# Two-layer decoder trunk on one core: the normalized stream by a diagonal product, products bank by bank, router and weight parts in another order

## What is computed

```python
h = rmsnorm(x, g) * (1.0 + scale) + shift   # rmsnorm: x * rsqrt(mean(x*x) + EPS) * g
x = x + gate * f(h)
# MoE: router logits, sigmoid, best 4 of 8 groups, best 8 experts, weights normalized
scores = sigmoid(h @ router_w)
y = sum over chosen e of w_e * (silu(h @ w1[e]) * (h @ w3[e])) @ w2[e]
y = y + (silu(h @ s_w1) * (h @ s_w3)) @ s_w2
```

## Time and profile before

| | |
|---|---|
| median of 3 runs | 1453.29 us (1452.13 to 1454.12) |
| the profiled execution | 1451.76 us, span 1450.0 us |
| busy: PE, DVE, ACT, POOL | 1328.0, 550.8, 444.5, 206.1 us |
| mean granted clock of TensorE | 0.974 of full speed |
| HBM read | 514.10 MB, 355 GB/s over the span |

### The profile page before, as it was taken

One profiled execution on the slowest core, in us unless ns is written; L12 is line 12 of the kernel. 1 busy time (PEld: TensorE's weight loads), 2 busy tenths in 40 slices (PEclk: granted clock), 3 DMA queues, 4 the chain that ended last, 5 costly groups with the idle time before them and its releaser, 6 DMA issues.

```text
span 1450.0 us, 32945 instructions
## 1 busy us (share of the span) xinstructions
PE 1328.0 (92%) x12029; PEld 875.3 (60%) x12030; DVE 550.8 (38%) x1217; ACT 444.5 (31%) x874; POOL 206.1 (14%) x657
## 2 busy tenths in 40 slices
PE   4899678999999999998789999789999999999996
PEld 2788366555455554554489989665555555555553
DVE  2565457233232332222443445473233223322333
ACT  3443333222122222221334454332222222222222
POOL 8000021111111111111000000011111111111110
PEclk9899988999999999999889999999999999999999
DMA  9999992999999999999985534529999999999994
GB/s 345 372 381 399 409 352 81 423 419 423 422 421 422 422 421 422 423 421 421 383 281 181 169 117 146 189 107 422 420 422 421 422 421 422 421 422 422 422 421 204
DMA packets 113082, 516.06 MB, mean 356 GB/s; under 512 B 9368, under 2 KB 46368, under 8 KB 63104
## 3 DMA queue, kind: packets, MB, share of 16 engines
q1 hardware_dynamic: 109920, 509.64, 87.6%
q0 software_dynamic: 2400, 3.49, 0.8%
q10 hardware_dynamic: 704, 2.10, 0.4%
HBM read 514.10 MB, written 1.09 MB: 355 GB/s over the span
## 4 chain that ended last, share of the span: by engine, by line
PE 72%; SPq 8%; DVE 5%; ACT 5%; DMA 5%; issue 3%; POOL 1%; ACTq 1%; DVEq 0%; POOLq 0%
PE bank L882 20%; PE bank L1059 15%; PE bank L1062 7%; PE bank L1080 7%; PE bank L994 6%; PE bank L1035 5%; SPq L336 5%; DMA ring<-in_exp_w_dram 4%; PE bank L1086 3%; PE bank L858 2%; SPq L339 2%; DVE arena L1487 1%; ACT arena L674 1%; DMA ring<-in_da_w_out_dram 1%; PE bank L1069 1%
## 5 line engine op out<-in xcount | busy, mean ns | idle before, releaser
L1059 PE MATMUL bank<-ring,arena 128*64 128x512 f32 x768 | 178.5, 605 | 13.1 <-DMA ring<-in_exp_w_dram 13.1
L1035 PEld LDWEIGHTS bank<-arena 128*128 128x128 bf16 x3264 | 142.1, 98 | 55.5 <-issue 55.0
L994 PE MATMUL bank<-arena_r 128*128 128x512 f32 x560 | 161.1, 418 | 3.0 <-DVE arena_r L1499 3.0
L1499 DVE TENSOR_TENSOR arena_r<-bank,arena_r 128x512 fp32r<-128x512 f32 x136 | 94.1, 692 | 154.1 <-ACT arena_r L686 154.1
L1035 PE MATMUL bank<-arena 128*128 128x64 bf16 (+1 forms) x3264 | 151.8, 207 | 0.0
L679 ACT ACTIVATE arena<-bank 128x256 f32<-128x256 f32 (+1 forms) x68 | 22.6, 333 | 386.9 <-PE bank L1059 269.8
L686 ACT CAST arena_r<-bank 128x512 fp32r<-128x512 f32 x136 | 79.7, 586 | 189.5 <-PE bank L1080 124.8
L994 PEld LDWEIGHTS bank<-arena_r 128*128 128x128 f32 x560 | 94.6, 188 | 60.0 <-issue 47.5
L882 PE MATMUL bank<-HH_r,ring_r 128*128 128x256 f32 x448 | 127.7, 285 | 0.0
L531 POOL TENSOR_TENSOR arena<-arena,pass_base 128x2 f32 x136 | 23.6, 197 | 732.2 <-PE bank L1046 727.1
L1059 PEld LDWEIGHTS bank<-ring,arena 128*64 128x64 f32 x768 | 56.5, 139 | 114.5 <-issue 113.9
(11 more groups left out here) (271 smaller groups left out, 2151.2 us busy)
## 6 DMA issues: line engine op xcount, KB each, us to landing
ring<-in_exp_w_dram SPq DMA_DIRECT2D x264, 1024.0 KB, 24.0
ring<-in_ada_w_dram SPq DMA_DIRECT2D x48, 1024.0 KB, 12.3
HH<-in_exp_w_dram SPq DMA_DIRECT2D x40, 1024.0 KB, 20.4
mods<-in_exp_w_dram SPq DMA_DIRECT2D x40, 1024.0 KB, 24.3
arena<-in_exp_w_dram SPq DMA_DIRECT2D x40, 1024.0 KB, 25.0
ring<-in_ret_w_in_dram SPq DMA_DIRECT2D x24, 1024.0 KB, 11.2
ring<-in_da_w_in_dram SPq DMA_DIRECT2D x12, 1024.0 KB, 16.4
ring<-in_ret_w_out_dram SPq DMA_DIRECT2D x8, 1024.0 KB, 4.9
```

The lines of the kernel that those rows point to most:

```text
L994: ins = nc.tensor.matmul(banks[4 + NH * tc + hf][:, :], S[:, P * tc:P * tc + P], y[:, r, 512 * hf:512 * hf + 512], start=False, stop=(last ...
L1035: ins = nc.tensor.matmul(banks[2 - 2 * half][:, P * kk:P * kk + 2 * W], parts[:, tc, r, P * (4 * half + kk):P * (4 * half + kk + 1)], Pg[: ...
L1059: ins = nc.tensor.matmul(banks[1][W * i:W * i + W, :], xg[:, k, W * i:W * i + W], w13[j][:, k, :, :], start=(k == 0), stop=(k == KD - 1))
L1499: nc.vector.tensor_tensor(y[:, 1, 512 * hf:512 * hf + 512], banks[hf][:, :], y[:, 0, 512 * hf:512 * hf + 512], ALU.subtract).then_inc(u[f" ...
```

## The change

1. **Turn.** DVE no longer scales x. It writes `diag`, 128x128 per token block, the identity times `rs`, and `turn_h` makes 16 true f32 products of `X` (read with a step of 8 elements) with `diag`. The first of them waits for POOL's identity alone (`ident_ready`); `pool_consts` gates the second half of the first `ada` step.
2. **Bank by bank.** ACT and DVE evict, round and split bank after bank, and the first products (router, or the first half of the first projection) wait for two blocks of the width at a time (`hT_there(k)`). In the first place ACT evicts bank 3 too, and the low part of the first weight tile stands between evictions.
3. **Router and weight parts.** The router weights are rounded and split during the output projection before. The first shared or projection tile's low part is made during the turn. Sigmoid and silu tables are loaded by dummy activations.
4. **Parts of x.** They are made from `X` and `rs`, per token block: the high part around the sigmoid, the rest only after `route_ready`, the third part after `shT`.
5. **Ranks.** The rank products stand ahead of the third half of shared up, the placing products ahead of the fourth; the weights come after at_rank. POOL writes the limits from `chosen_ready` on and no longer clears `y`.

```diff
+        diag = ret_s[:, 0:TC * P].rearrange("p (c t) -> p c t", c=TC)
...
+                def round_high(m):
+                    if m in by_act:
+                        act.wait_ge(hT_act, (2 * n + 1 if n else 0) + by_act.index(m) + 1)
                     else:
-                        act.wait_ge(hT_dve, 2 * n + m // 2 + 1)
+                        act.wait_ge(hT_dve, (2 * n - 1 if n else 0) + by_dve.index(m) + 1)
                     nc.scalar.copy(hT_hi[:, 2 * m:2 * m + 2, :], hT_full[:, 2 * m:2 * m + 2, :]).then_inc(hT_rounded, 1)
+
+                act.wait_ge(mod_T_in[n], 1 if n == 0 else 16)
+                evict(0)
+                round_high(0)
+                evict(2)
+                round_high(1)
+                if n == 0:
+                    evict(3)
+                round_high(2)
+                round_high(3)
...
             def moe(l):
+                if l == 1:
+                    load_root_table()
                 round_w("shared", l, 0)
                 norm_stats()
-                act.wait_ge(late_consts_in, 16 * 5)
-                nc.scalar.copy(rw_hi, rw[:, :, :]).then_inc(rw_rounded, 1)
+                round_w("shared", l, 1)
+                nc.scalar.activation(lexp[:, 0:1], ident[:, 0:1], ACT.Sigmoid)
                 evict_hT()
-                round_w("shared", l, 1)
-                nc.scalar.copy(parts[:, :, 0, :], h).then_inc(part_hi, 1)
+
+                def part_high(tc):
+                    nc.scalar.activation(parts[:, tc, 0, :].rearrange("t (k p) -> t k p", k=KD),
+                                         X[:, tc, :].rearrange("t (p k) -> t k p", k=KD), ACT.Copy, scale=rs[:, tc:tc + 1]
+                                         ).then_inc(part_hi, 1)
+
+                part_high(0)
                 act.wait_ge(logits_done, l + 1)
-                nc.scalar.activation(scoreT, banks[2][:, 0:T], ACT.Sigmoid).then_inc(scoresT_ready, 1)
-
-                act.wait_ge(rest_ready, l + 1)
-                nc.scalar.copy(parts[:, :, 1, :], h).then_inc(part_mid, 1)
+                nc.scalar.activation(scoreT, banks[0][:, 0:T], ACT.Sigmoid).then_inc(scoresT_ready, 1)
+                part_high(1)
+                nc.scalar.activation(lexp[:, 0:1], ident[:, 0:1], ACT.Silu)
+                for tc in range(TC):
+                    act.wait_ge(rest_ready, TC * l + tc + 1)
+                    nc.scalar.copy(parts[:, tc, 1, :], h[:, tc, :]).then_inc(part_mid, 1)
...
             def turn_h():
                 for tc in range(TC):
-                    pe.wait_ge(h_ready, TC * norms[0] + tc + 1)
+                    pe.wait_ge(diag_ready, TC * norms[0] + tc + 1)
                     for m in range(4):
                         for kk in range(2):
-                            ins = nc.tensor.transpose(
-                                banks[m][:, T * kk + P * tc:T * kk + P * tc + P],
-                                h[:, tc, P * (2 * m + kk):P * (2 * m + kk + 1)], ident[:, :])
+                            ins = nc.tensor.matmul(banks[m][:, T * kk + P * tc:T * kk + P * tc + P],
+                                                   X[:, tc, :].rearrange("t (p k) -> t k p", k=KD)[:, 2 * m + kk, :],
+                                                   diag[:, tc, :], start=True, stop=True)
                         if tc == TC - 1:
                             ins.then_inc(h_turned, 1)
                 norms[0] += 1
 
-            def hT_there():
-                pe.wait_ge(hT_split, 4 * norms[0])
+            def hT_there(k):
+                if k % 2 == 0:
+                    pe.wait_ge(hT_split, 4 * (norms[0] - 1) + k // 2 + 1)
...
                 for k in range(KD):
+                    if i == 0 and m == 0:
+                        hT_there(k)
...
             def moe(l):
                 turn_h()
-                hT_there()
                 pe.wait_ge(rw_split, l + 1)
 
                 for k in range(KD):
-                    ins = product(banks[2][:, 0:T], (rw_hi[:, k, :], rw_lo[:, k, :]), [x[:, k, :] for x in hTs],
+                    hT_there(k)
+                    ins = product(banks[0][:, 0:T], (rw_hi[:, k, :], rw_lo[:, k, :]), [x[:, k, :] for x in hTs],
                                   k == 0, k == KD - 1)
                 ins.then_inc(logits_done, 1)
...
+                    if i == 1:
+                        pe.wait_ge(chosen_ready, l + 1)
+                        nc.tensor.matmul(banks[3][:, 0:E], upper[:, :], mb[:, 0, :], start=True, stop=True)
...
+                            pe.wait_ge(at_rank_ready, l + 1)
+                            nc.tensor.matmul(banks[3][0:1, 4 * E:5 * E], expert_id[:, 0:1], at_rank, start=True, stop=True)
+                            nc.tensor.matmul(banks[3][0:1, 5 * E:6 * E], count_own[:, 0:1], at_rank, start=True, stop=True
+                                             ).then_inc(experts_placed, 1)
...
-                pe.wait_ge(at_rank_ready, l + 1)
...
+                if n == 0:
+                    dve.wait_ge(ident_ready, 1)
                 if not last:
                     for tc in range(TC):
-                        nc.vector.tensor_scalar(h[:, tc, :].rearrange("t (k p) -> t k p", k=KD),
-                                                X[:, tc, :].rearrange("t (p k) -> t k p", k=KD), rs[:, tc:tc + 1], None, ALU.mult
-                                                ).then_inc(h_ready, 1)
+                        nc.vector.tensor_scalar(diag[:, tc, :], ident[:, :], rs[:, tc:tc + 1], None, ALU.mult).then_inc(diag_ready, 1)
...
+                dve.wait_ge(mod_T_in[n], 1 if n == 0 else 16)
+                evict(1)
+                if n == 0:
+                    low_part("mix_in", 0, 0)
+                low(0)
+                if n > 0:
+                    evict(3)
+                for m in range(1, 4):
+                    low(m)
...
             def moe(l):
                 norm_root()
-                dve.wait_ge(rw_rounded, l + 1)
-                nc.vector.tensor_tensor(rw_lo, rw[:, :, :], rw_hi, ALU.subtract).then_inc(rw_split, 1)
+                low_part("shared", l, 0)
                 evict_hT()
-                low_part("shared", l, 0)
-
-                dve.wait_ge(h_turned, 4 * norms[0])
-                dve.wait_ge(part_hi, l + 1)
-                nc.vector.tensor_tensor(h, h, parts[:, :, 0, :], ALU.subtract).then_inc(rest_ready, 1)
                 low_part("shared", l, 1)
+
+                def rest_part(tc):
+                    dve.wait_ge(part_hi, TC * l + tc + 1)
+                    nc.vector.scalar_tensor_tensor(out=h[:, tc, :].rearrange("t (k p) -> t k p", k=KD),
+                                                   in0=X[:, tc, :].rearrange("t (p k) -> t k p", k=KD), scalar=rs[:, tc:tc + 1],
+                                                   in1=parts[:, tc, 0, :].rearrange("t (k p) -> t k p", k=KD),
+                                                   op0=ALU.mult, op1=ALU.subtract).then_inc(rest_ready, 1)
+
+                def low_rest_part(tc):
+                    dve.wait_ge(part_mid, TC * l + tc + 1)
+                    return nc.vector.tensor_tensor(parts[:, tc, 2, :], h[:, tc, :], parts[:, tc, 1, :], ALU.subtract)
...
-                dve.wait_ge(part_mid, l + 1)
-                nc.vector.tensor_tensor(parts[:, :, 2, :], h, parts[:, :, 1, :], ALU.subtract).then_inc(parts_ready, 1)
...
                 nc.vector.tensor_scalar(npass, npf, 1.0, None, ALU.add).then_inc(route_ready, 1)
+                rest_part(0)
+                rest_part(1)
+                dve.wait_ge(sh_silu, l + 1)
+                nc.vector.tensor_tensor(shT, sg.rearrange("p (b t) -> p b t", b=2),
+                                        banks[1][:, :].rearrange("p (b t) -> p b t", b=2), ALU.mult).then_inc(sh_ready, 1)
+                low_rest_part(0)
+                low_rest_part(1).then_inc(parts_ready, 1)
...
             low_part("mix_out", 0, 3)
+            split_rw(0)
             dve.wait_ge(gates_in, 32)
             update_x(2, ((first_rows_out, 1), (out_done, 4)))
...
             norm_root()
+            low_part("mix_in", 1, 0)
             evict_hT()
```

More of the change, by code:

```diff
@@ L308, in trunk @@
         proj0_bank = {i: banks[7 * (n % 2)] for n, (kind, i) in enumerate(turns) if kind == "proj"}
-        proj1_bank = {i: banks[3 + (i % 4 if i < 16 else (i + 1) % 2)] for i in range(24)}
+        proj1_bank = {i: banks[3 + ((i + 1) % 4 if i < 16 else (i + 1) % 2)] for i in range(24)}
         ada_bank = {k: banks[7 * (n % 2)] for n, (kind, k) in enumerate(turns) if kind == "ada"}
@@ L1347, in evict_hT, with low @@
                     ins.then_inc(hT_dve, 1)
-                for m in range(4):
+                def low(m):
                     dve.wait_ge(hT_rounded, 4 * n + m + 1)
@@ L1661, in low_yT @@
                 nc.vector.tensor_tensor(low, full, ret_yT[:, :, hd, :], ALU.subtract).then_inc(oT_split, 1)
-            for i in range(17):
+            for i in range(1, 17):
                 low_part("mix_in", 1, i)
```

113 lines of the change are left out of this document (55 added, 58 removed).

## The result

| | before | after |
|---|---|---|
| median | 1453.2 us (4 runs, 1452.13 to 1454.12) | 1515.43 us (4 runs, 1513.56 to 1517.19) |
| ratio | | 1.043, 95% interval 1.0414 to 1.0446 |
| span of the profiled execution | 1450.0 us | 1515.5 us |
| mean granted clock | 0.974 | 0.958 |

The change makes the kernel 62 us slower, where -1.7 us was forecast with a range up to 1456.6. PE is busy for 30 us more and the span is 65.5 us longer.

The account below looks back on a forecast made before the run. PE is busy 1328 of 1450 us, and both routed loops keep the DMA full at 421 GB/s. Start -1.9, MoE entries +4.4 and retention -4.2 sum to -1.7 us: 1451.6 us, 8-in-10 range 1446.8 to 1456.6.

Parts of the forecast that it names:

- each MoE entry is worth what it moves the end of the shared down product: Both routed loops: loop and weight stream hang on shared down's end; +2.2 us per entry, +4.4 for two.
- C: Rival: the turn is slower than its columns say, loads at 0.43 us a row; +13.2 us, 1464.8, chance 0.07.
- signs of being wrong: PE gap before shared down under 2 us, or L900 over 0.25 us a row, would show the forecast wrong.
- Rounding and splitting the router weights ... price 0: Moved under the output projection, where ACT and DVE pause: price 0, or 1.15 us each if that cover went.
- 32 rows by 0.21 = 6.8 us: Turn of x: f32 products at half clock take 6.8 us for 3.7, bounds 4.8 and 7.7; first eviction 1.0 later.
- Products bank by bank: After the turn: first pair starts 2.3 us after the first eviction, where products began 5.0 us after it.
- The rests are now in front of the shared product: MoE entry: two rests, 2.5 us, on the path; net +0.5 us, and PE waits some 3.8 us before shared down.
- The price of 1.7: Each MoE entry: half clock behind PE's longer wait costs 8.76 - 7.04 = 1.7 us, bounds 0 and 3.4.
- Rival B: The clock stays up in the wait before shared down, or the wait is shorter: 3.4 us less, 1448.2, chance 0.32.
- Retention -4.2: Before the retention projections: first products at 726.0 instead of 730.18, all kept; -4.2 us, bounds -2.2 and -5.
- Start -1.9: Kernel start: products at 37.0 instead of 40.82, the mixer's DMA taking over about 1.9 us; bounds 0 and -3.7.
- First loop +1.7: First routed loop: the prediction put 0 for this step; +1.7 us is the measured value.

Follow-up runs that it names:

- e1_before_pad: Kernel before with 130 more long-satisfied waits in PE's program and nothing else: 1506.3 us, ratio 1.0354.
- e2_after_pad: Changed kernel with 64 more long-satisfied waits in PE's program ahead of the second routed loop: 1463.63 us, ratio 1.0063 to the kernel before.
- e8_after_pad8: Changed kernel with only 8 more waits in PE's program ahead of the second routed loop: 1462.82 us, ratio 1.0068 to the kernel before.
- e4_rw_back: Changed kernel with 64 added waits, first layer's router weights rounded and split behind the norm again: 1458.52 us, ratio 1.0034 to the kernel before.
- e6_transposes: Changed kernel with the old turn (DVE scales x, PE makes 16 transposes), no added waits: 1459.6 us, ratio 1.0037 to the kernel before.
- e7_three_transposes: Changed kernel, old turn, silu and shared product before rests, first-layer router weights behind norm, weights' parts earlier, no added waits: 1444.02 us, ratio 0.993.

## Why the prediction was wrong

**The loops: "each MoE entry is worth what it moves the end of the shared down product".** The step that failed is the first one of the working: it took the routed loops as unchanged but for when they start, so the sum has no term for them. 16 f32 products in place of 16 transposes are 32 more instructions in each turn of x (16 more rows of products and 16 more loads of their stationary side), 128 over the four turns, and with 2 waits more this moved the second loop's code by 130. That was 52 of the 62 us. The profile of the kernel before could have raised the question (q8's 44 packets, six in the loop's first turn and then none), but the prediction counted the new rows in time alone, never in code. None of its rivals, C included, has this mechanism. e1_before_pad, e2_after_pad and e8_after_pad8 show it with nothing else changed. The prediction's own signs of being wrong stayed silent: the gap before shared down was over 2 us, and L900 at 0.248 us a row just under 0.25. They watched only the terms that had been priced.

**"Rounding and splitting the router weights ... price 0".** Wrong: +4.2 us. The working priced DVE's and ACT's time and looked for pauses; it did not ask for what the copy has to wait. POOL issued its five late loads before and after at nearly the same time (from 191.3 and from 190.4), and the last lands at 209.2, after the place to which the copy was moved. Before, ACT's copy ran behind the norm, when all five had landed. e4_rw_back gives 5.1 us back.

**"32 rows by 0.21 = 6.8 us", first eviction 1.0 us later.** The mechanism was right, the term too small: 7.9 us, and 5.3 us to the first eviction where 4.3 was put. Rival C named the cause, the read with a step of 8, and gave it the price of 0.43 us a row; it is 0.25 (7.9/32), under C's turning point of 0.29. The row that was set against C, 128 small products with the same step, did not carry over to 128 columns. The rule of the Trainium skill (Perfetto Trace Analysis, "Transposes"), which the prediction weighed and set aside, is right for this kernel: e6_transposes and e7_three_transposes are each 3 to 4 us faster than their like with the diagonal. In the sum it would have been 9 us, which no run shows; whether the start of the products by pairs gives back the rest was not run by itself.

**"Products bank by bank", forecast first pair at +2.3.** Close: +2.7 (first eviction 223.95, first product 226.66). The scores were copied 13.5 us behind the root (231.67 less 218.14), before 16.0; forecast were 12.6. The missing 0.9 us is about what the turn took more up to the first eviction (1.0).

**"The rests are now in front of the shared product".** Right as a mechanism, too small by their price: STT rows of the final scaling, 1.24 us each, stood for them, but L1421 takes 2.1 us each, 4.15 for both; it reads X with the step of 8, which the row that stood for it does not. No run changes that read alone. The wait before L1017 was 5.0 us (forecast 3.8), and shared down took 10.16 us in the first entry and 9.22 in the second for 7.13, so the half clock cost 3.0 and 2.1 us and not 1.7, within the bound of 3.4. The price of 1.7 compared 30 rows with 32; row for row it is 2.2. Rival B is refuted, as the clock fell with shared down:

```profile
248.60:255.40 6.80, 6.12 (x7) 2.52 (x8) 4.49 (x7) 0.00 (x0) 2.02 (x6) 0.50 0.69 288
```

Both entries: +5.8 and +5.2 for +2.2 each.

**Retention -4.2.** Right in kind: -3.1. The slower turn (7.9 us for 6.8) is as long as the difference.

**Start -1.9.** -0.7 in the profiled execution. In the seven kernels with this start (the kernel after and six of the runs) the first mixer ended between 206.2 and 210.4, before at 210.0. The lead at the first products (37.5 in the kernel after, 40.8 before) was there in all of them, 2.9 to 3.7 us, but what was left of it at the end differed, from -3.8 to +0.4, about the bounds of -3.7 and 0.

**First loop +1.7.** Not explained. In e8_after_pad8, whose code for this loop is the same, it is gone: the time from the end of shared down to PE's last gather is 451.4 us there, 452.8 in the kernel after and 451.1 before. So it is not a fixed price of the change.

**Slips in the working.** The last bank comes 12 rows by 0.21, so 2.5 us, behind the first, not 2.3, and B with the best bound of the start is 1446.4, not 1446.8. Neither would have changed the forecast.

Without the code's place the kernel would still have been slower, by 8 to 10 us (e2_after_pad and e8_after_pad8). The sign was lost on three terms, the size on the one that had no term.

## What to carry to other kernels

Before a change is costed in time, count its instructions on every engine that runs a long loop, and ask in which fetched block that loop then starts: the profile's instruction queue tells whether a loop fits (packets in the first turn, none after), and a handful of harmless instructions ahead of it tests it, whatever else was edited. A step moved earlier is free only if its inputs are there by then, so look for the landing of each DMA that its semaphore counts, and not for pauses of the engine. And price an instruction by a row with the same access pattern, not only the same size.

## What the runs showed of the hardware

- A loop of 1594 instructions on PE ran without fetches or with nine 16 KB fetches in every turn, by where it started. A back edge then cost 10.8 us (two blocks in a row, 5.4 us each beside weight loads at over 400 GB/s) and the granted clock was 0.50 for 10 to 14 us from inside the wait on: 13 us a turn in all (52.1/4).
- A true f32 product with its stationary side read with a step of 8 elements takes 0.24 us a row at either clock; with adjacent elements 0.138 at 2.4 GHz and 0.208 at 1.2.
- Rows of ACT and DVE that read X with the same step were longer as well: on ACT 128x1024 scaled from X to bf16 (L667) took 2.3 us, a copy of the same size from adjacent elements (L678) 1.05; on DVE it was 2.1 us (L1421) against 1.24. These are different operations, and no run changes the step alone.
